# Unused fp32r matmuls around the scores of each head, in the attention of the first two mixers

## The reference, cut to what matters

```python
# even mixer: 8 heads of width 64, causal, with a decay term F
s = jnp.einsum('bqhd,bkhd->bhqk', qb, k) * (dh ** -0.5)
s = s + (Fb.transpose(0, 2, 1)[..., :, None] - F_keys[..., None, :])
s = jnp.where(key_pos[None, :] <= q_pos[:, None], s, -jnp.inf)
o = jnp.einsum('bhqk,bkhd->bqhd', jax.nn.softmax(s, axis=-1), v)
# odd mixer: 16 heads of width 64, keys chosen by an index score, with a bias;
# the same three steps: scores, softmax, probabilities times values
```

## Time and profile before

| | |
|---|---|
| median of 3 runs | 2106.26 us (2106.0 to 2118.86) |
| the profiled execution, first to last instruction | 2110.7 us |
| TensorE busy | 1946.6 us (92%), mean granted clock 0.923 |
| `even` attention, first scores to first output projection | 324.03 to 369.40 us |
| `odd` attention, the same | 913.91 to 976.86 us |
| other engines busy | DVE 66%, ACT 44%, POOL 36% |

### The profile page before, as it was taken

How to read it: one execution, slowest core, us unless ns; L and a number is a source line. 1 busy time by engine, 2 the same in 40 slices (tenths; PEclk the granted TensorE clock), 3 DMA queues, 4 the chain that set the end, 5 groups by cost and what they waited for, 6 DMA issues and landing times.

```text
span 2110.7 us, 34770 instructions
## 1 busy us (share of the span) xinstructions
PE 1946.6 (92%) x14460; PEld 1844.3 (87%) x14460; DVE 1394.3 (66%) x1393; ACT 919.1 (44%) x1168; POOL 764.3 (36%) x392
## 2 busy tenths in 40 slices
PE   7999999799989999999799987898999896989998
PEld 7999895699989999857799986788999886889997
DVE  6877544676767776554777759956555589666554
ACT  5444453344434434343333342564444444745443
POOL 3967000346657674020566739700000079000000
PEclk9999896899989998967899988899999998999998
DMA  7877341368676765511477733333655332344551
GB/s 235 270 238 244 98 145 55 100 215 265 227 220 200 256 223 178 179 41 56 154 249 238 243 100 100 111 113 117 188 179 191 120 126 94 121 140 151 180 188 41
DMA packets 288106, 347.61 MB, mean 165 GB/s; under 512 B 15060, under 2 KB 263688, under 8 KB 288008
## 3 DMA queue, kind: packets, MB, share of 16 engines
q1 hardware_dynamic: 287976, 346.18, 50.7%
q10 hardware_dynamic: 32, 0.02, 0.0%
HBM read 345.11 MB, written 1.07 MB: 164 GB/s over the span
## 4 chain that ended last, share of the span: by engine, by line
PE 77%; DVE 16%; ACT 4%; issue 1%; SPq 1%; DMA 1%; ACTq 0%; DVEq 0%
PE bank L765 22%; PE bank L766 22%; PE bank L767 22%; DVE arena L1927 4%; DVE wl L1597 4%; ACT wh L1244 2%; PE bank L940 2%; PE bank L963 2%; DVE xl L1608 1%; DVE xn L1628 1%; PE bank L951 1%; PE bank L1201 1%; PE bank L802 1%; DVE hl L1658 1%; DMA raw<-in_ffn_w_in 1%
## 5 line engine op out<-in xcount | busy, mean ns | idle before, releaser
L1597 DVE TENSOR_TENSOR wl<-raw,wh 128x2048 fp32r<-128x2048 f32 x275 | 736.1, 2682 | 384.3 <-ACT wh L1244 384.2
L765 PE MATMUL bank<-xh,wh 128*128 128x256 f32 x3056 | 889.0, 291 | 70.7 <-DVE xl L1608 33.5
L766 PE MATMUL bank<-xl,wh 128*128 128x256 f32 x3056 | 880.3, 288 | 0.0
L767 PE MATMUL bank<-xh,wl 128*128 128x256 f32 x3056 | 879.7, 288 | 0.0
L1244 ACT ACTIVATE wh<-raw 128x2048 fp32r<-128x2048 f32 x275 | 524.8, 1909 | 403.6 <-PE bank L767 388.0
L765 PEld LDWEIGHTS bank<-xh,wh 128*128 128x128 f32 x3056 | 603.1, 197 | 88.1 <-issue 54.5
L766 PEld LDWEIGHTS bank<-xl,wh 128*128 128x128 f32 x3056 | 603.3, 197 | 0.4 <-issue 0.2
L767 PEld LDWEIGHTS bank<-xh,wl 128*128 128x128 f32 x3056 | 602.7, 197 | 0.0
L707 POOL TENSOR_TENSOR arena<-arena,csil 128x2048 f32<-128x2048 f32 x48 | 185.3, 3859 | 505.3 <-DMA arena<-in_w_ada 486.2
L765 PE MATMUL bank<-hh,wh 128*128 128x256 f32 x1216 | 348.7, 287 | 16.7 <-DVE hl L1658 16.7
L766 PE MATMUL bank<-hl,wh 128*128 128x256 f32 x1216 | 348.0, 286 | 0.0
(11 more groups left out here) (253 smaller groups left out, 1714.2 us busy)
## 6 DMA issues: line engine op xcount, KB each, us to landing
raw<-in_ffn_w_in SPq DMA_DIRECT2D x88, 1024.0 KB, 5.8
arena<-in_w_ada SPq DMA_DIRECT2D x48, 1024.0 KB, 7.5
raw<-in_ffn_w_out SPq DMA_DIRECT2D x44, 1024.0 KB, 5.0
raw<-in_w_in SPq DMA_DIRECT2D x36, 1024.0 KB, 5.0
raw<-in_w_up SPq DMA_DIRECT2D x32, 1024.0 KB, 5.7
raw<-in_w_down SPq DMA_DIRECT2D x32, 1024.0 KB, 4.9
raw<-in_even_w_in SPq DMA_DIRECT2D x12, 1024.0 KB, 5.3
raw<-in_w_out SPq DMA_DIRECT2D x8, 1024.0 KB, 5.1
```

Source lines behind the costliest of these rows:

```text
L765: pe.matmul(o, wa, ma, start=start, stop=False, **kw)
L766: pe.matmul(o, wa, mb, start=False, stop=False, **kw)
L767: return pe.matmul(o, wb, ma, start=False, stop=stop, **kw)
L1597: dve.tensor_tensor(wl[:, c % RING, :], raw[:, c % RING, :], wh[:, c % RING, :].bitcast(F32), ALU.subtract).then_inc(lo_made.sem, 1)
```

## The change

`fill(3)` is called twice in each turn of `pe_attention`, before and after the place of the scores, in `even` and in `odd`. It issues three fp32r matmuls, stationary tile 128 x 128, moving tile 128 x 512, both from the chunk that `wh` holds for the output projection, into bank 2, whose content nobody reads. It is called in all H+3 turns, also in those without scores. Before the first turn there are two more waits: for the last projection's copy out of its bank, and for the rounding of the chunk that is read. In the `mix` mixers nothing is added.

```diff
@@ -963,9 +963,21 @@
+            def fill(count):
+
+                for _ in range(count):
+                    pe.matmul(bank[2][:, :], wh[:, held, 0:P], wh[:, held, 0:512], start=True, stop=True)
+
+            fillers = 0 if KIND[s] == "mix" else 3
+            held = (base[s] + (12 if s == "even" else 7)) % RING
+            if fillers:
+                pe.wait_ge(proj_out.sem, proj_out.at(s))
+                pe.wait_ge(hi_made.sem, base[s] + (12 if s == "even" else 7) + 1)
             for i in range(H + 3):
+                fill(fillers)
                 if i < H:
                     scores(i)
+                fill(fillers)
                 if meanwhile:
                     meanwhile(i)
                 if 2 <= i < H + 2:
```

## The result

The changed kernel has a median of 2117.28 us over 20 runs (2113.63 to 2132.96), the kernel before 2110.28 over 20 (2105.7 to 2121.01). The medians are 7.0 us apart; the ratio is 1.0042 with a 95% interval of 1.0025 to 1.0058, about 9 us slower (5 to 12): within 1%, the median inside the range 2096 to 2126, and more than the 2.3 us of the forecast. Four of the 20 runs lie above 2126. The first line is the changed kernel's busy time by engine, which answers to the earlier trace rows; its mean granted clock is 0.948 where it was 0.923.

A forecast was written before the change was run, and what follows sets the result against it. TensorE, busy 92% of the span and at half clock in both attentions, was taken as the bound. Terms -1.9 (`even`), -0.35 (`odd`) and +4.6 (lapses) gave +2.3 us on 2106.3: 2108 us, range 2096 to 2126.

The forecast's parts named there:

- The clock: TensorE in both attentions: fillers lift it from 0.50; `even` heads 6.04 to 4.85 us, `odd` 3.88 to 3.62.
- The first rival: Both attentions: the clock isn't lifted and stays at 0.50 with fillers; 2195 us in all; chance 0.06.
- the working: Time at 0.50 throughout with fillers: `even` 80.2 us (+34.8), `odd` 117.2 us (+54.2), whole 2195 us.
- The filler's price: Each `fill` call: 3 x 0.227 + 0.10 = 0.78 us at the upper clock, 1.45 at the lower; two a turn.
- a switch: Extra time of the first fp32r matmul after scores: 0.10 us at the upper clock, 0.17 at the lower.
- the sum: Both attentions: `even` 43.5 us (-1.9), `odd` 62.6 us (-0.35) at the upper clock, lapses +4.6; together +2.3 us.
- the rival of cheap fillers: Fillers at 0.214 us with switches hidden: 2096 us; with weight loads also hidden, 2086; chance 0.05.
- The lapses: `even`: 10 us at the lower clock, costing +4.6 us, falling within the first two heads; none in `odd`.
- The second rival: `even`: clock wavers, lower for half of the heads' work; attention 61.9 us (+16.5), whole 2122 us; chance 0.13.

The follow-up runs named there:

- the two halves: Change's fillers in one mixer only, against the kernel before: `odd` alone 2113.4 us, ratio 1.0011; `even` alone 2115.19 us, ratio 1.0019.

## Why the prediction was right, and where a size was off

**The clock.** It was right that the fillers lift it, all through `odd` and for most of `even`, and, as TensorE had no gap in the later heads, that it is not by closing gaps; the run with 8 rows shows that it is what they put into the array. The first rival (0.50 throughout) had nearly the right price: the run with 8 rows is 85 us slower where the working gives 89. That it meets the 2195 us of the working so closely is luck: `odd` takes 117.3 us for 117.2 only because heads of 7.03 us for 6.78 are set off by its start at 1.00 and its cheaper last turns, and `even` takes 70.3 us where the working gives 80.2. The reading of the Trainium skill ("TensorE: Matmul & The Clock Gate", "The HAM clock gate") by which a busy TensorE has its full clock is contradicted by that run, in which it was busy for 6.00 of 6.00 us at 0.50.

**The filler's price.** Its terms were a little small: 0.24 us a filler where I took 0.227, and a switch behind an output of 0.89 - 3 x 0.24 = 0.17 us, where I took the 0.10 that rows show behind scores. The two calls cost 1.69 us in a turn with scores and transposes, not 1.56, and about as much as forecast where they follow one another (1.49 to 1.60). Heads came out accordingly: 4.98 us for 4.85, 3.76 for 3.62. At 1.00 throughout `odd` took 64.28 us where the sum has 62.6, 1.7 more. `even` took 45.54; its lapse cost 1.3 us in the fillers and 0.2 in the scores behind, so without it 44.0, 0.5 more than the 43.5 of the sum. Together that is about 2.2 us of the 6.6 between the forecast (+2.3) and the measurement (about +9). The 131 ns a matmul at 512 columns that the Trainium skill gives (same page, "Back-to-back issue gap") is not borne out by the 0.24 us here, and the rival of cheap fillers falls with it.

**The lapses.** This is the term that was mis-sized most. The sum had 10 us at the lower level in `even`, a cost of 4.6 us. The change's profile has one lapse of 3 to 4 us, right at the start as forecast, and the run with `even` alone shows a profile with 27 us at 0.50 in one stretch and 3 more later. The mean over the runs can be had in two ways, both estimates. What the price leaves over is 4.4 us, so the lapses cost about 9 us in place of 4.6, some 20 us at 0.50. And each execution has its mean granted clock: 0.948 in the profiled one and 0.9443 in the mean of the 20. With two levels only, 0.0037 less over 2112 us is 0.0037 x 2112 / 0.50 = 16 us more at 0.50 than in the profiled one, again about 20 with its own lapse. That they lie in `even` is shown by the profiles and the spread of the two halves (`odd` alone: eleven of twelve runs within 8 us), not for each execution. So the forecast had the right cause with half its size; that the median still fell well inside the range is owed to a range of 30 us. The second rival (`even` wavering, +16.5) is what single executions do, not the median.

**What I did not ask.** The sum was right that in `odd` nearly all that the clock brings back goes into the fillers, and stopped there. It priced a head at 1.00 without fillers (2.06 us) and never asked whether the later heads need them to stay there. They don't: 15 fillers at the start do for `odd` what 114 did (as far as mean clocks tell, in all six runs with fillers at its start alone and in seven of the eight with fillers at both starts), and the saving of 21 us that the forecast held to be eaten is there.

## What to carry to other kernels

A full busy column says nothing of the clock: read the granted clock beside it, and compare a loop's length with the same loop elsewhere in the trace at the other level. Where dense filler work lifts the clock, first find where it fell (here a start of thin matmuls; closing the wait in it with more of them did not help) and whether the loop holds its level by itself afterwards; pay for the lift once, and not in every turn. Where the loop doesn't hold it, as in the profiles of `even`, filler in every turn has to be set against its own time: here three in a call took 45.5 us for 45.4 in a good execution and 57.8 in a bad one, and five 54.3. And take several executions: one profile can miss the lapses that make the mean.

## What the runs showed of the hardware that was not expected

The same `odd` loop of fp32 matmuls ran at either level for its whole length, 2.1 to 2.7 us a head at 1.00 and 3.88 us at 0.50, by how it began. At 1.00 it had waits (4.71 of 5.00 us busy) and kept the level, and at 0.50 it had none and didn't rise in its heads. Nor does the clock need a wait to fall: with fillers of 8 rows it fell within 5 us of `odd`'s first filler, TensorE having work all the time. An fp32r matmul of 512 columns costs 0.24 us at 1.00, twice one of 256, so nothing is saved by the longer one. Matmuls of 8 rows do not count for the clock as those of 128 do, at the same number of columns: 0.50 with the first and 1.00 with the second. And a filler of 8 rows and a decay matmul of 8 rows started 0.01 us apart (345.19 and 345.18), where each takes 0.79 us.
